# First chunk of each layer reordered, with a later Toeplitz store and narrower or wider sum steps, in a two-layer hybrid decoder step

## What is computed

```
def hybrid_layer(x, C0, n0, m0, S0, k_buf, v_buf, pos0, norm_gain, w_in, ...):
    u = rms_norm(x, norm_gain)
    proj = jnp.einsum('btd,dc->btc', u, w_in).astype(f32)
    h_m, C, n, m = mlstm(...)                       # chunks of 128 tokens, gated state
    h_r, S = retention(rope(...), rope(...), ...)   # chunks of 128 tokens, decaying state
    h_a, kw, vw = window_attention(...)             # window of 128, shared T5 relative bias
    mix = jnp.concatenate([out_m, out_r, out_a], axis=-1)
    return x + jnp.einsum('btc,cd->btd', mix, w_out), ...
```

## Time and profile before

| what | value |
|---|---|
| median of three runs | 2082.65 us |
| profiled execution, its own time | 2080.63 us |
| its span | 2078.8 us |
| PE busy | 2006.7 us (97% of the span) |
| DVE busy | 1655.4 us (80%) |
| ACT busy | 885.5 us (43%) |
| POOL busy | 333.4 us (16%) |
| mean granted PE clock | 0.983 |

### The profile page before, as it was taken

How to read it: one execution, slowest core, us unless ns; L and a number is a source line. 1 busy time by engine, 2 the same in 40 slices (tenths; PEclk the granted TensorE clock), 3 DMA queues, 4 the chain that set the end, 5 groups by cost and what they waited for, 6 DMA issues and landing times.

```text
span 2078.8 us, 36212 instructions
## 1 busy us (share of the span) xinstructions
PE 2006.7 (97%) x12814; PEld 1129.6 (54%) x12814; DVE 1655.4 (80%) x3968; ACT 885.5 (43%) x2270; POOL 333.4 (16%) x320
## 2 busy tenths in 40 slices
PE   5799999999999999999979999999999999999997
PEld 3465655555555555445446555555555555554453
DVE  7788888888888888675566888888888888887866
ACT  6744444444444446231265444444444444452100
POOL 2011111111111122120010111111211111111200
PEclk9899999999999999999999999999999999999999
DMA  9212111111211114885631112111121111357542
GB/s 318 65 37 53 43 52 42 42 42 45 58 42 42 42 46 130 181 252 152 220 104 36 43 44 59 43 42 42 42 53 42 48 45 42 102 138 183 141 123 91
DMA packets 256531, 174.89 MB, mean 84 GB/s; under 512 B 216087, under 2 KB 230104, under 8 KB 256284
## 3 DMA queue, kind: packets, MB, share of 16 engines
q1 hardware_dynamic: 240452, 142.14, 26.7%
q0 software_dynamic: 7424, 29.43, 4.0%
q10 hardware_dynamic: 8568, 2.18, 0.5%
HBM read 85.29 MB, written 42.29 MB: 61 GB/s over the span
## 4 chain that ended last, share of the span: by engine, by line
PE 87%; DVE 7%; ACT 3%; issue 1%; DMA 1%; POOL 0%; SPq 0%; DVEq 0%; ACTq 0%
PE J L574 53%; PE J L1286 14%; PE W L978 3%; PE W L989 2%; PE W L1061 1%; PE W L1091 1%; ACT W L558 1%; PE W L1079 1%; PE W L1050 1%; DVE W L565 1%; PE J L1025 1%; PE T L1070 1%; PE W L964 1%; PE W L996 1%; PE T L1035 1%
## 5 line engine op out<-in xcount | busy, mean ns | idle before, releaser
L574 PE MATMUL J<-W,x_mix 128*128 128x512 f16 (+2 forms) x3072 | 609.4, 355 | 5.9 <-ACT PB L1406 3.9
L574 PE MATMUL J<-W,uT_mix 128*128 128x512 f16 (+2 forms) x3072 | 609.9, 356 | 3.4 <-ACT PB L1406 3.4
L574 PEld LDWEIGHTS J<-W,x_mix 128*128 128x128 f16 x3072 | 298.5, 99 | 277.4 <-issue 14.1
L574 PEld LDWEIGHTS J<-W,uT_mix 128*128 128x128 f16 x3072 | 299.2, 99 | 273.9 <-issue 6.9
L1406 ACT ACTIVATE PB<-J,out_scale 128x512 f32<-128x512 f32 (+2 forms) x256 | 154.5, 603 | 303.3 <-PE J L574 294.9
L1376 ACT ACTIVATE ST<-ST,small 128x1024 f16<-128x1024 f32 x32 | 36.7, 1148 | 206.2 <-DVE small L1880 206.2
L1286 PE MATMUL J<-W,EM_qkR_mix 128*128 128x512 f16 x480 | 115.4, 379 | 0.0
L2328 POOL TENSOR_TENSOR ST<-ST,ge 128x512 f32<-128x512 f32 x32 | 67.8, 2118 | 218.3 <-DVE ST L1864 218.3
L1370 ACT ACTIVATE sc_xr<-sc_xr,small 128x128 f32<-128x128 f32 x256 | 98.6, 389 | 0.0
L1286 PE MATMUL J<-W,x_mix 128*128 128x512 f16 x400 | 98.5, 386 | 0.0
L1286 PE MATMUL J<-W,uT_mix 128*128 128x512 f16 x400 | 98.2, 385 | 0.0
(11 more groups left out here) (472 smaller groups left out, 3510.2 us busy)
## 6 DMA issues: line engine op xcount, KB each, us to landing
W<-in_w_in POOLq DMA_DIRECT2D x8, 2048.0 KB, 12.9
mix_d<-ST SPq DMA_DIRECT2D x32, 512.0 KB, 2.6
sc_xr<-in_x_prompt SPq DMA_DIRECT2D x20, 512.0 KB, 4.2
sc_xr<-x SPq DMA_DIRECT2D x20, 512.0 KB, 3.8
ST<-in_w_in POOLq DMA_DIRECT2D x4, 2048.0 KB, 12.5
W<-in_w_out SPq DMA_DIRECT2D x4, 2048.0 KB, 8.2
PB<-in_x_prompt SPq DMA_DIRECT2D x6, 512.0 KB, 3.8
x<-PB SPq DMA_DIRECT2D x6, 512.0 KB, 3.5
```

Of the source, the lines that this page charges most:

```text
L574: mm = nc.tensor.matmul(out, stationary(k, a), moving[:, k, b, :], start=(k == 0 and n == 0), stop=(k == KT - 1 and n == 2))
```

## The change

The order of steps in the first chunk of both layers is written anew, on four engines:

- PE, layer 0: `spread_rows` and `r_turn` stand behind `sample_block` of block 3 rather than before it.
- ACT, layer 0: `evac_first(1)` ahead of `block_sum(4)`, `block_hi(4)` cut in two halves around `rows_exp`, `evac_sample(3)` ahead of `block_sum(6)`. At the very start the sample's root comes ahead of `block_sum(0)`.
- DVE, layer 0: `rows_in` ahead of `block_top(4)`, `rows_scan` ahead of `block_max(5)`, `block_lo(4)` cut around `rows_out`, `top_of_all(5)` ahead of `tokens`.
- Layer 1: `block_scale(3)` ahead of the sample's norm (at the end of `output_dve`), `block_hi(3)` and `block_hi(4)` cut, `evac_sample(0)`, `(1)` spread between, `block_scale(5)` ahead of `tokens`, `block_hi(5)` behind `evac_sample(3)`, and `block_sum(6)` behind `evac_first(4)`.
- Blocks 5, 6 and 7 of layer 1 get two wide sums in place of six. The unread result of wide sums goes to the tile `PB`, where it waits in layer 1 for the last store of the output ring's first buffer.
- SP: the Toeplitz store is issued after the sample stores of block 4 (`p == 4`) rather than of block 0, and `load_bias` no longer waits for the sums. The sample rows are loaded second, the identity matrix fourth. POOL waits for the first prompt rows before it loads block 1.

```
@@ SP @@
             sp.dma_start(x_first[0], A["x_prompt"][0][0:CHUNK, :]).then_inc(E["x_loaded"], 16)
-            sp.dma_start(ident, A["c128"][:, 0:P]).then_inc(ident_loaded, 16)
             sp.dma_start(xs, A["x_sample"].rearrange("b t d -> (b t) d")).then_inc(S["x"], 16)
             load_gain(sp, 0)
+            sp.dma_start(ident, A["c128"][:, 0:P]).then_inc(ident_loaded, 16)
...
-                if layer == 0 and p == 0:
+                if layer == 0 and p == 4:
                     store_toeplitz(sp)
                 if layer == 0 and p == 6:
-                    sp.wait_ge(C["sum_ready"], sums_before(layer, NBLK))
                     load_bias(sp)
@@ sums @@
-        SUM_GROUPS = [2, SUM_KS]
+        def sum_groups(layer, j):
+            return SUM_KS if layer and j <= INSIDE + 1 else 2
...
-            unread = bias[:].rearrange("p h c -> p (h c)").bitcast(BF16)[:, 0:rows.shape[1] * rows.shape[2]]
+            unread = PB[:].bitcast(BF16)[:, 0:rows.shape[1] * rows.shape[2]]
@@ PE @@
-                if p == 3:
+                if layer and p == 3:
                     spread_rows(n)
                     r_turn(n, B[0])
...
                 sample_block(p, 1)
+                if layer == 0 and p == 3:
+                    spread_rows(n)
+                    r_turn(n, B[0])
@@ ACT, both layers, behind block 3 @@
             v_hi(0, P0 + 3)
+            evac_sample(3, 1)
+            if layer:
+                block_hi(act, layer, 5)
+                evac_first(4, 0)
             block_sum(act, layer, 6)
-            evac_sample(3, 1)
             gate_log(n, "r")
             if layer == 0:
                 block_hi(act, layer, 5)
-            evac_first(4, 0)
+                evac_first(4, 0)
```

More of the change, by code:

```diff
@@ L443, in build @@
         SUM_KS, WO_SUMS = 6, 6
-        SUM_GROUPS = [2, SUM_KS]
         sums = [0]
+        def sum_groups(layer, j):
+            return SUM_KS if layer and j <= INSIDE + 1 else 2
         def sums_before(layer, j):
-            return SUM_GROUPS[layer] * j + (SUM_GROUPS[0] * NBLK + 2 * WO_SUMS if layer else 0)
+            return sum(sum_groups(layer, i) for i in range(j)) + (sums_before(0, NBLK) + 2 * WO_SUMS if layer else 0)
         def abs_sum(act, out, row):
@@ L471, in block_sum @@
             act.wait_ge(w_loaded[b], 16 * (layer + 1))
-            for i in range(SUM_GROUPS[layer]):
-                if layer == 0:
+            wide = sum_groups(layer, j) == 2
+            if wide:
+                wait(act, o_stored[0], 16 * layer * SLOT_TILES[0])
+            for i in range(sum_groups(layer, j)):
+                if wide:
                     abs_sum_wide(act, wmax[:, j, SUM_KS - 2 + i:SUM_KS - 1 + i], raw(layer, b)[:, 3 * i:3 * i + 3, :])
@@ L494, in block_top @@
             dve.wait_ge(C["sum_ready"], sums_before(layer, j + 1))
-            first = SUM_KS - SUM_GROUPS[layer]
+            first = SUM_KS - sum_groups(layer, j)
             st(V.tensor_reduce(wmax[:, j, SUM_KS + 1:KT], wmax[:, j, first:SUM_KS + 1], AX.X, ALU.max))
@@ L550, in block_scale, with block_hi @@
                 V.tensor_scalar(v_scale[:, 1:2], wm[:, 1:2], 2.0 ** -14 / (V_SCALE * U_SCALE * P_SCALE), None, ALU.mult)
-        def block_hi(act, layer, j):
+        def block_hi(act, layer, j, ks=range(KT)):
             b = SAMPLE_ORDER[j]
@@ L556, in block_hi @@
             wait(act, C["lo"], KT * (NBLK * layer + j))
-            for k in range(KT):
+            for k in ks:
                 nc.scalar.activation(pair[b][:, k, 0, :], raw(layer, b)[:, k, :], ACT.Copy, scale=gs[:, j, k:k + 1]
@@ L1500, in prompt_act @@
                 block_sum(act, layer, 5)
+                evac_sample(2, 1)
+                block_hi(act, layer, 4, range(0, 4))
                 rows_exp(n)
-                evac_sample(2, 1)
-                block_hi(act, layer, 4)
+                block_hi(act, layer, 4, range(4, KT))
             else:
@@ L1506, in prompt_act @@
                 act.wait_ge(prompt_stored, 16 * 9 * layer)
+                block_hi(act, layer, 3, range(0, 4))
                 sample_rstd(act, layer)
-                block_hi(act, layer, 3)
+                block_hi(act, layer, 3, range(4, KT))
                 evac_first(0, 0)
+                block_sum(act, layer, 5)
                 sample_uT_hi()
                 evac_first(1, 1)
-                block_sum(act, layer, 5)
+                evac_first(2, 0)
                 rows_log(n)
-                evac_first(2, 0)
+                evac_sample(0, 1)
+                block_hi(act, layer, 4, range(0, 4))
+                evac_sample(1, 0)
                 rows_exp(n)
-                evac_sample(0, 1)
-                evac_sample(1, 0)
-                block_hi(act, layer, 4)
                 evac_sample(2, 1)
-                block_hi(act, layer, 5)
+                block_hi(act, layer, 4, range(4, KT))
             evac_first(3, 0)
@@ L2061, in prompt_dve @@
                 block_max(dve, layer, 5)
+                block_scale(dve, layer, 4)
+                rows_in(n)
                 block_top(dve, layer, 5)
[L2063 to L2064 removed]
                 rows_scan(n)
+                top_of_all(dve, layer, 5)
+                block_lo(dve, layer, 4, range(0, 3))
                 rows_out(n)
[L2067 to L2068 removed]
+                block_lo(dve, layer, 4, range(3, KT))
+                block_scale(dve, layer, 5)
                 tokens(n)
[L2070 removed]
                 block_lo(dve, layer, 5)
@@ L2297, in output_dve @@
                 dve.wait_ge(Q["y_added"], 2 * TILES * L1)
+                block_scale(dve, layer + 1, 3)
                 sample_norm(dve, layer + 1, xr[CHUNKS % RING][0:TS, :])
```

25 lines of the change are left out of this document (12 added, 13 removed).

## The result

The changed kernel takes 2096.49 us (median of 7 runs), the kernel before 2081.56 us (median of 7). One of the seven runs was disturbed (8938.03 us) and is left out of the ratio; without it the median is 2094.0 us. The ratio is 1.0058, 95% interval 1.0038 to 1.0079: slower by 0.58%, where 2085 us, about 0.1% more than the 2082.65 us then known, was forecast. The first median lies half a microsecond above the upper end of the range (2096 us), the second inside it. The profiled execution took 2091.54 us, 10.9 us more than that of before.

What follows compares the result with a forecast made beforehand. PE was taken to bound the kernel, through its second-chunk starts in both layers. Layer 0 +7.2 and layer 1 -4.7 make +2.5 on 2080.63, 2083.1 us; with the median 2.0 above the profiled run, 2085 us, range 2072 to 2096.

Steps and rivals of the forecast that it cites:

- Layer 1, -4.7 us: Layer 1's first chunk: reordered steps walked at -4.2 us, one slow-clock stall less -0.5; range -7 to -2.
- First chunk of layer 0 without the store: Layer 0, reordered steps if nothing else stood in the way: second chunk starts 6.3 us sooner, at 107.5 in the walk.
- start: SP's first loads and POOL's wait: -0.7 us at the head of the chain, range -1 to +0.5; PE starts at 12.2.
- The store's time: Toeplitz store in its new place: takes 33.5 us (30 to 37), issued at 77.8, ends at 111.3.
- the store is no bar: Rival: with DMA engines free the store runs twice as fast, ends by 98 us; -11.8, 2071 us; chance 0.13.
- The rows: Load of layer 0's second-chunk rows, behind the store in SP's queue: lands at 108.3, second chunk 11.2 us later at 119.5.
- ACT's order: Layer 0: ACT's gate exponential, ready at 98.6, waits 12.7 us for the store; second chunk 5.3 us after the store's end.
- The slow clock: Layer 0: PE resumes at slow clock after its idle stretch, 2.6 us against 1.6 before; net +1.5, range 0 to +3.
- near 121: Sign to look for in the new trace: PE's second chunk in layer 0 starts near 121 us.
- Rows last: Rival: queue served in order, store takes 37 us, rows land at 118.8, chunk at 130.1; +13.1, 2096 us; chance 0.15.
- Rows not late: Rival: the second chunk's rows land by 105 us, only the gate wait counts; 2083 us; chance 0.20.
- layer 1 does not gain: Rival: the new 4.5 us wait at top_turn(6) brings the slow clock, layer 1 gives 0; +7.2, 2090 us; chance 0.14.

Runs made afterwards that it cites:

- the two-step store: Changed kernel, Toeplitz store in its new place but as 8 rows to DRAM, then DRAM to DRAM with 128 copies outermost: 2069.38 us, ratio 0.9942.
- the kernel with the old start: The two-step store's kernel with SP's first loads, order of norm and sums, and POOL's missing wait as in the kernel before: 2069.62 us.
- the move alone: The kernel before with only the Toeplitz store moved, from behind block 0's sample stores to behind block 4's: 2103.97 us, ratio 1.0114.

## Why the prediction was right and where it was wrong

- **PE bounds, and the two chunk starts decide: right.** +13.96 and -4.48 us make +9.5 of 10.9.
- **Layer 1, -4.7 us: right, -4.5.** From the layer's first transposes on, the high parts of block 5 start 2.4 us sooner (walked 2.6), the load of block 7 is released 2.4 us sooner (walked 3.1), and `top_turn(6)` waits 4.4 (walked 4.5).
- **First chunk of layer 0 without the store: right in size.** 6.3 walked and 0.8 of clock, 7.8 measured with the two-step store; `top_spread` at most 3.9 us where 4.2 was walked. The **start** in it was mis-sized: -0.7 taken, 2.0 measured. I held the constants to stand behind the same bytes; with POOL's second load held back to 5.56 us PE began at 10.0 instead of 12.2, and in the kernel with the old start at 11.4. Which of the undone parts did it is not shown.
- **The store's time: right,** 34.8 us from issue to end where 33.5 was taken, issued at 77.21 (77.8), over at 111.97 (111.3). But the reasoning on it was thin: I took 32 pieces a us from the lone stretch and named the number of engines as the reason. The rival "the store is no bar" would have been worth a question about the source.
- **The rows, the step that failed.** "I take 3 us before the store's end, between the two rows": they landed 1.7 us after it, in the changed kernel and (122.1 against 120.5) in the move alone. 113.6 instead of 108.3 is +5.3 us. The misreading is in the earlier trace rows. The two sample stores of a block count up one semaphore, 16 steps each, and the landing times there are read off that count. In the trace of before half of the steps came early and half at the end: 32 pieces of 1024 bytes moved at 53.5 to 53.9 us and 32 at 56.3 to 56.6, after each of the two was issued, and the other 64 at 71.3 to 73.2. So the "14.0" is when both stores had half of their pieces through, and neither had landed before the Toeplitz store's end near 73 us. There was no early row to take the middle with. A 512 KB load of 128 pieces is split in the same way (64 pieces at 97 to 99 us, 64 from 111.5 on), and it is complete only with its later half.
- **The issue of the rows, missed without harm.** It was put near 98 and came at 91.65, since the stores of block 5 took SP 7.95 us and not the 12.5 of the old place. The rows stood behind the store all the same.
- **ACT's order, missed.** I had ACT wait 12.7 us for `toep_stored`; it waited for the second chunk's norm ahead of that, which the walk did not hold. That it cost nothing was luck, since rows and store ended together.
- **The slow clock, under-sized.** From PE's resumption to the second chunk 9.7 us passed where the two-step kernel took 5.8, 3.9 more, and 0.9 in its first blocks: 4.8. The sum had +1.5 net of the 1.6 in the old chunk, so 3.1. The sign "near 121" left these 1.6 out; the prediction's own +7.2 gives 115.36 + 7.2 = 122.6. With the rows at 113.6, the walked 11.2 us and 3.9 of clock make 128.7; measured 128.45. So rows (+5.3) and clock (+1.7) explain layer 0: 7.2 + 7.0 = 14.2, measured 13.96.
- **The rivals.** "Rows last" describes the rows: what spreads over all engines and is issued behind the store in its queue is complete only at its end. Its price for layer 0 (+17.8) was too high, since it gave the store 37 us and the rows 4 more, where 34.8 and 1.7 were measured. That its 2096 us is close to the measured medians is in part chance. "Rows not late" is refuted, "the store is no bar" became true once its source was changed, and "layer 1 does not gain" is refuted. That rows last was held for unlikelier than a middle between two rows is the error of judgement, and it came from the early row that was none.
- **The sum.** +7.2 for layer 0 against +13.96, -4.7 against -4.5. Hence 2083.1 forecast for the profiled execution and 2091.54 measured: 8.4 us too low, 6.8 of it layer 0. The slight loss that was forecast was smaller than the 10.4 us that the prediction itself says can be told from no change. The time stayed at the upper end of the range because the range reached to the price of the rows-last case, and not because the sum was close.

A version that beats both kernels came out of it: the new order with the store from 128 partitions (2067.17 us) or over DRAM (2067.69 us), 0.9% below the kernel before by the ratios, and some 1.5% below the changed one, an estimate from two ratios to before that were not measured side by side. What each of the reordered steps gives by itself was only walked, and no run takes them apart.

## What to carry to other kernels

When a bulk transfer is moved away from a busy stretch, ask which DMA engines it holds and for how long, and then treat every transfer that needs those engines and stands behind it in its queue as landing at its end; another queue brought the rows only 4 us forward here. A landing time read off a semaphore that two transfers share does not say which of them has landed. Before moving it, ask why it is slow: here 1.6 MB out of 8 partitions took 34.8 us, and the same bytes out of 128 took 6.3, and with a store of 9.4 us over DRAM its place hardly mattered. And where a walk of the engines is made "without" a step, the walk should also be made with that step in its old place, since a faster order can run into what the slow one hid.

## What the runs showed of the hardware

The price of a piece depends on how many partitions the source spreads over. 1600 bytes took 224 ns when eight engines read from 8 partitions (51 GB/s in all), 69 ns when sixteen read from 128 (385 GB/s), and 82 ns when seven read from DRAM (132 GB/s). The Trainium skill, "SBUF — State Buffer", section "Door 1: The DMA port swizzle", has a rule that fits: DMA reaches SBUF by 16 ports of four and four partitions, and partitions 0 to 7 lie on two of them. By that page's figure for all ports, 436 GB/s, two carry 54 GB/s, an estimate that the measured 51 comes close to.

The kernel before has a row that speaks for a limit that the eight share. While the weights took part of the engines' time, 58 to 60 us, the same pieces from the same partitions took 0.223 x 16 x 2 / 64 = 112 ns, and still only 32 came through each microsecond:

```profile
q1 hardware_dynamic: 64, 0.10, 22.3%
```

So reading one partition again and again is not what costs 224 ns, which the 69 ns of the 128 partitions, each of them read 8 times, bear out; the rate of all eight together is what stays. That it is the ports that set it is not shown: no run here read from 8 partitions that lie apart. The rule on the ports was the one to weigh in the prediction, more than the one on the outermost dimension.

A transfer over all engines behind the confined one is split: 64 of the rows' 128 pieces moved at 97 to 99 us and the rest only when the store was done. In another queue the pieces take turns with the store's instead, and the load still landed late (109.6, the store's end at 109.8). And the idle stretch of PE of 17.8 us was paid for once more: the granted clock of 118 to 132 us was 0.53.
